# A seven-product feed-forward kernel: five couples of weight rows in each wide pair instead of four

## The reference

```python
f = jnp.square(jax.nn.relu(rms_norm(x, g_ffn_pre) @ w_up)) @ w_down
return x + rms_norm(f, g_ffn_post)
```

## Time and profile before

| | |
|---|---|
| median of 3 runs | 1889.78 us (1889.22 to 1890.29) |
| the profiled execution | 1889.38 us |
| its span | 1887.3 us |
| busy: PE, PE weight load, DVE, ACT | 99%, 89%, 79%, 59% |
| layer 0: feed-forward groups 0, 1, 2, 3 start their wide pairs at | 378.3, 539.8, 701.3, 863.2 us |

### The profile page before, as it was taken

One profiled execution on the slowest core, in us unless ns is written; L12 is line 12 of the kernel. 1 busy time (PEld: TensorE's weight loads), 2 busy tenths in 40 slices (PEclk: granted clock), 3 DMA queues, 4 the chain that ended last, 5 costly groups with the idle time before them and its releaser, 6 DMA issues.

```text
span 1887.3 us, 27369 instructions
## 1 busy us (share of the span) xinstructions
PE 1874.9 (99%) x9950; PEld 1672.1 (89%) x9950; DVE 1497.9 (79%) x1885; ACT 1111.4 (59%) x1485; POOL 118.5 (6%) x166
## 2 busy tenths in 40 slices
PE   9999999999999999999999999999999999999998
PEld 7988988988988998898888888889889889989987
DVE  6886657898699689788877757678977996897886
ACT  6455656855665565566554556568556655645662
POOL 3920010000000000000000000100000000000000
PEclk9999999999999999999999999999999999999999
DMA  8665366757566666767576554586676666567673
GB/s 290 201 221 181 112 201 226 236 182 255 189 198 216 214 198 195 236 202 241 210 234 225 187 168 134 170 275 194 197 236 207 195 212 221 183 207 235 221 257 124
DMA packets 170068, 390.92 MB, mean 207 GB/s; under 512 B 12161, under 2 KB 14321, under 8 KB 168433
## 3 DMA queue, kind: packets, MB, share of 16 engines
q1 hardware_dynamic: 167904, 377.58, 61.8%
q10 hardware_dynamic: 2064, 12.08, 1.7%
HBM read 382.53 MB, written 7.08 MB: 206 GB/s over the span
## 4 chain that ended last, share of the span: by engine, by line
PE 95%; DVE 3%; issue 1%; ACT 0%; DMA 0%; POOL 0%; DVEq 0%; POOLq 0%; ACTq 0%
PE acc_pair L573 25%; PE acc_pair L578 13%; PE acc_pair L539 8%; PE acc_pair L540 8%; PE acc_pair L541 8%; PE acc_pair L874 7%; PE acc_pair L873 7%; PE acc_pair L872 7%; DVE w_lo L1445 1%; PE t_bank L874 1%; PE t_bank L873 1%; PE t_bank L872 1%; PE o_bank L791 1%; DVE h_both L1501 1%; PE ssa_bank L872 1%
## 5 line engine op out<-in xcount | busy, mean ns | idle before, releaser
L995 ACT CAST w_hi<-raw 128x1024 fp32r<-128x1024 f32 x687 | 703.6, 1048 | 476.4 <-DVE raw L1998 190.7
L1445 DVE TENSOR_TENSOR w_lo<-raw,w_hi 128x1024 fp32r<-128x1024 f32 x687 | 827.4, 1232 | 169.0 <-ACT w_hi L995 161.8
L573 PE MATMUL acc_pair<-h_both,w_hi 128*128 128x512 f32 x2176 | 560.3, 380 | 0.2
L573 PEld LDWEIGHTS acc_pair<-h_both,w_hi 128*128 128x128 f32 x2176 | 371.4, 190 | 30.4 <-issue 0.5
L578 PEld LDWEIGHTS acc_pair<-h_both,w_lo 128*128 128x128 f32 x2176 | 327.4, 190 | 29.2
L578 PE MATMUL acc_pair<-h_both,w_lo 128*128 128x256 f32 x2176 | 330.5, 274 | 0.0
L872 PE MATMUL acc_pair<-w_hi,f_hi 128*128 128x512 f32 x504 | 191.0, 379 | 0.0
L873 PE MATMUL acc_pair<-w_lo,f_hi 128*128 128x512 f32 x504 | 191.0, 379 | 0.0
L874 PE MATMUL acc_pair<-w_hi,f_lo 128*128 128x512 f32 x504 | 191.0, 379 | 0.0
L539 PE MATMUL acc_pair<-w_hi,h_both 128*128 128x512 f32 x444 | 170.4, 384 | 1.8 <-DVE w_lo L1445 1.6
L540 PE MATMUL acc_pair<-w_lo,h_both 128*128 128x512 f32 x444 | 168.3, 379 | 0.0
(11 more groups left out here) (252 smaller groups left out, 2293.8 us busy)
## 6 DMA issues: line engine op xcount, KB each, us to landing
raw<-in_w_up SPq DMA_DIRECT2D x256, 512.0 KB, 4.4
raw<-in_w_down SPq DMA_DIRECT2D x240, 512.0 KB, 5.0
raw<-in_w_in SPq DMA_DIRECT2D x128, 512.0 KB, 4.7
raw<-in_w_out SPq DMA_DIRECT2D x64, 512.0 KB, 5.3
raw_side<-in_w_down SPq DMA_DIRECT2D x16, 512.0 KB, 7.0
x_kept<-x ACTq DMA_DIRECT2D x4, 1024.0 KB, 6.2
x<-x_kept ACTq DMA_DIRECT2D x4, 1024.0 KB, 6.1
x<-in_x SPq DMA_DIRECT2D x8, 256.0 KB, 7.5
```

The source lines that it names most:

```text
L573: pe.matmul(acc_pair[b][:, m, :], w_hi[:, slot, col:col + P], x_both.rearrange("p s (a n) -> p s n a", a=2), start=(slot, k) == (0, 0), st ...
L995: act.copy(w_hi[:, half * PAIRS + p, :], raw[:, p, :]).then_inc(hi_made, 1)
L1445: dve.tensor_tensor(w_lo[:, slot, :], src[:, p, :], w_hi[:, slot, :].bitcast(F32), ALU.subtract).then_inc(lo_made, 1)
```

## The change

Each wide pair has five couples of seven products and three plain ones. In the first pair of a group they are at slots 0, 4, 6, 10 and 12, in the second at 0, 4, 8, 12 and 14. Their activation rows come from up units 0 to 2, so there are no activation sums in the last unit, and one more set per group; in group 0 the sums of unit 0 are read from PSUM. The weight sums are formed by other formulas in another order: first the difference that goes back into `raw` (`weight_third`, now waiting for both loads), then one sum of 512 columns, then one subtraction 1024 wide. Where a couple follows a couple, `weight_third` of the next stands ahead of `t_lo`. The four shared banks are one tensor; in groups 0 and 1 ACT copies them out, in groups 2 and 3 DVE adds them in one instruction 2048 wide. In group 0 ACT also reads the banks of the first pair. In the last up unit DVE makes the second square, and prepares slots 0 to 5 instead of 0 to 7. At the end of a second pair the bank sums stand between low parts of the next unit.

```diff
-SEVEN_AT = (0, PAIRS, RING, RING + PAIRS)
-SEVEN_UNIT = ((1, 0), (1, 1), (2, 0), (2, 1))
-K_ORDER = (4, 5, 0, 1, 6, 7, 2, 3, 8, 9, 12, 13, 10, 11, 14, 15)
+SEVEN_AT = ((0, 4, 6, 10, 12), (0, 4, 8, 12, 14))
+COUPLES = tuple(len(at) for at in SEVEN_AT)
+LAYER_COUPLES = FF_GROUPS * COUPLES[0] + (FF_GROUPS - 1) * COUPLES[1]
+SEVEN_UNIT = ((0, 0), (0, 1), (1, 0), (1, 1), (2, 0))[:max(COUPLES)]
+PLAIN_LAST = tuple(SLOTS - 2 not in at for at in SEVEN_AT)
 SHARED = 4
+def k_order(q):
+    pairs = [4 * u + 2 * b for u, b in SEVEN_UNIT[:COUPLES[q]]]
+    plain, order = iter([k for k in range(0, KT, 2) if k not in pairs]), []
+    for i in range(0, SLOTS, 2):
+        k = pairs[SEVEN_AT[q].index(i)] if i in SEVEN_AT[q] else next(plain)
+        order += [k, k + 1]
+    return order
+K_ORDER = (k_order(0), k_order(1))
...
-    t_bank = [nc.alloc_psum_tensor(f"t_bank{n}", [P, CH], F32) for n in range(2)]
-    o_bank = nc.alloc_psum_tensor("o_bank", [P, CH], F32)
-    ssa_bank = nc.alloc_psum_tensor("ssa_bank", [P, CH], F32)
+    shared = nc.alloc_psum_tensor("shared", [P, SHARED, CH], F32)
+    ssa_bank, t_bank, o_bank = shared[:, 0, :], [shared[:, 1, :], shared[:, 2, :]], shared[:, 3, :]
...
-                    pe.wait_ge(lo_made, (hu + i // PAIRS) * PAIRS + 2 + RAW)
+                    pe.wait_ge(lo_made, (hu + i // PAIRS) * PAIRS + i % PAIRS + 2 + RAW)
...
-                        three(t_bank[1][:, :], sh[:, 0, :], sl[:, 0, :], th[:, 0, :], tl[:, 0, :],
+                        three(o_bank[:, :], sh[:, 1, :], sl[:, 1, :], th[:, 0, :], tl[:, 0, :],
                               begin, end).then_inc(t_used, 1)
-                        three(o_bank[:, :], sh[:, 1, :], sl[:, 1, :], th[:, 1, :], tl[:, 1, :],
+                        three(t_bank[1][:, :], sh[:, 0, :], sl[:, 0, :], th[:, 2, :], tl[:, 2, :],
                               begin, end).then_inc(t_used, 1)
                     if first:
...
-                          th[:, 2, :], tl[:, 2, :], first, False).then_inc(t_used, 1)
+                          th[:, 1, :], tl[:, 1, :], first, closing).then_inc(t_used, 1)
...
+                def two_hi(g, q, i):
+                    hu = hu0 + HU_F + g * HU_GROUP + 2 * CHUNKS + PAIR_HALVES * q + i // PAIRS
+                    if i in SEVEN_AT[q]:
+                        act.wait_ge(t_third, seven_no(l, g, q, SEVEN_AT[q].index(i)) + 1)
+                    split_hi(hu, i // PAIRS % 2, (i % PAIRS, i % PAIRS + 1))
+                def wide_hi(g, q, begin, end=SLOTS):
+                    for i in range(begin, end, 2):
+                        two_hi(g, q, i)
+                        if i in SEVEN_AT[q]:
+                            sums_hi(g, q, SEVEN_AT[q].index(i))
...
+                def first_shared(g):
+                    if g == 0:
+                        act.wait_ge(x_saved, 16 * T * (l + 1))
+                    act.wait_ge(t_used, 3 * seven_no(l, g, 0, COUPLES[0]) - 1)
+                    for k in range(SHARED):
+                        act.copy(kept_sums[:, 1 - pair_at(g, 0), k, :], shared[:, k, :]
+                                 ).then_inc(shared_free, 1)
...
+                def first_sums():
+                    act.wait_ge(rstd_ready, T + l * RS_LAYER + RS_X2 + T)
+                    for t in range(T):
+                        for c in range(2):
...
+                            dst = halves(acc[:, t, c_cols(2 * pair_at(0, 0) + c)])
+                            act.mul(dst, put_back(acc_pair[t][:, c, :]),
+                                    rstd[:, COL_X2 + t:COL_X2 + t + 1]).then_inc(acc_free[t], 1)
...
-                    seven_hi(g, 0, 2, hu + 10, 0)
-                    seven_hi(g, 0, 3, hu + 11, 1)
+                    last_unit(g)
+                    wide_hi(g, 0, 6)
                     if not last:
-                        for n in range(PAIR_HALVES):
-                            seven_hi(g, 1, n, hu + 12 + n, n % 2)
+                        wide_hi(g, 1, 0, 2)
+                        if g < T:
+                            first_shared(g)
+                        two_hi(g, 1, 2)
+                        if first:
+                            first_sums()
+                        wide_hi(g, 1, 4)
...
+                def last_square(g):
+                    z = act_f[:, 1, :]
+                    dve.wait_ge(acc_free[1], 1 + a0 + ACC_F + g * 8 + CHUNKS)
+                    dve.scalar_tensor_tensor(z, z, 0.0, z, ALU.max, ALU.mult
+                                             ).then_inc(f_ready, 1)
...
+                def weight_third(g, q, n):
+                    i = SEVEN_AT[q][n]
+                    hu = hu0 + HU_F + g * HU_GROUP + 2 * CHUNKS + PAIR_HALVES * q + i // PAIRS
+                    top_r, low_r = (raw[:, i % PAIRS + m, c_cols(1)] for m in range(2))
+                    for m in range(2):
+                        dve.wait_ge(raw_loaded[i % PAIRS + m], hu * 16 + 16)
+                    dve.tensor_tensor(top_r, low_r, top_r, ALU.subtract).then_inc(t_third, 1)
+                def weight_sums(g, q, n):
+                    no, i = seven_no(l, g, q, n), SEVEN_AT[q][n]
+                    top = raw[:, i % PAIRS, :]
+                    low = raw[:, i % PAIRS + 1, :].rearrange("p (c n) -> p c n", c=2)
+                    out = t_sum[t_buffer(q, n)]
+                    if q * COUPLES[0] + n > 1:
                         dve.wait_ge(t_used, 3 * no - 5)
+                    elif l + g > 0:
+                        dve.wait_ge(t_used, 3 * seven_no(l, g, 0, 0))
                     elif n == 1:
                         dve.wait_ge(tables_saved, 32)
-                    dve.wait_ge(raw_loaded[0], hu * 16 + 16)
-                    dve.tensor_tensor(out[:, 0, :], top_r, top_l, ALU.subtract
+                    dve.wait_ge(t_third, no + 1)
+                    dve.tensor_tensor(out[:, 0, :], top[:, c_cols(1)], top[:, c_cols(0)], ALU.add
                                       ).then_inc(t_step, 1)
-                    dve.wait_ge(raw_loaded[1], hu * 16 + 16)
-                    dve.tensor_tensor(top_r, low_r, top_r, ALU.subtract).then_inc(t_third, 1)
-                    dve.wait_ge(t_step, 3 * no + 1)
-                    if again:
-                        dve.wait_ge(t_used, 3 * no - 4)
-                    dve.tensor_tensor(out[:, 1, :], low_r, out[:, 0, :], ALU.subtract
-                                      ).then_inc(t_step, 1)
-                    dve.wait_ge(t_step, 3 * no + 2)
-                    if again:
+                    dve.wait_ge(t_step, 2 * no + 1)
+                    if q * COUPLES[0] + n > 1:
                         dve.wait_ge(t_used, 3 * no - 3)
-                    dve.tensor_tensor(out[:, 2, :], low_l, out[:, 1, :], ALU.subtract
-                                      ).then_inc(t_step, 1)
+                    dve.tensor_tensor(out[:, 1:3, :], low, out[:, 0:1, :].to_broadcast([P, 2, CH]),
+                                      ALU.subtract).then_inc(t_step, 1)
...
+                def couple_lo(g, q, i):
+                    n = SEVEN_AT[q].index(i)
+                    weight_sums(g, q, n)
+                    two_lo(g, q, i)
+                    if i + 2 in SEVEN_AT[q]:
+                        weight_third(g, q, n + 1)
                     sums_lo(g, q, n)
-                    split_lo(hu, half, (2, 3))
+                def wide_lo(g, q, begin):
+                    for i in range(begin, SLOTS, 2):
+                        if i not in SEVEN_AT[q]:
+                            two_lo(g, q, i)
+                            continue
+                        if i - 2 not in SEVEN_AT[q]:
+                            weight_third(g, q, SEVEN_AT[q].index(i))
+                        couple_lo(g, q, i)
...
-                    for k, bank in enumerate((ssa_bank, t_bank[0], t_bank[1], o_bank)):
-                        dst = kept_sums[:, 1 - j, k, :]
-                        if g < T:
-                            dve.tensor_copy(dst, bank[:, :]).then_inc(shared_free, 1)
-                        else:
-                            dve.tensor_tensor(dst, bank[:, :], dst, ALU.add
-                                              ).then_inc(shared_free, 1)
+                    dve.wait_ge(t_used, 3 * seven_no(l, g, 0, COUPLES[0]) - 1)
+                    dve.wait_ge(shared_free, shared_done(l, g - T))
+                    dst = kept_sums[:, 1 - pair_at(g, 0), :, :]
+                    dve.tensor_tensor(dst, shared[:, :, :], dst, ALU.add
+                                      ).then_inc(shared_free, SHARED)
...
-                    hu = hu0 + HU_F + g * HU_GROUP + 2 * CHUNKS + PAIR_HALVES * q
-                    seven_lo(g, q, 2, hu + 2, 0)
-                    seven_lo(g, q, 3, hu + 3, 1)
-                    nxt = hu + PAIR_HALVES
+                    nxt = hu0 + HU_F + g * HU_GROUP + 2 * CHUNKS + PAIR_HALVES * (q + 1)
+                    wide_lo(g, q, (6, 4)[q])
                     if q == 0 and not last:
-                        weight_sums(g, 1, 0, nxt)
```

(37 more changed lines are left out.)

209 lines of the change are left out of this document (115 added, 94 removed).

## The result

The changed kernel takes 1927.32 us (median of 4 runs, 1926.58 to 1931.76) against 1889.97 for the kernel before in the same session: a ratio of 1.0203, 95% interval 1.0185 to 1.0221. The sign was forecast, the size was not: +37 us where I had said +11, and outside my range. The profiled execution has a span of 1925.8 us, against 1887.3.

What follows compares the result with a forecast made beforehand. PE bounds the kernel (busy 99%), with DVE close behind. 9.1 us of matmuls go, DVE's lateness costs 10.2 us a layer, 20.4 in two: 1889.4 - 9.1 + 20.4 = 1900.7, about 1901; range 1881 to 1908.

Steps and rivals of the forecast that it cites:

- What goes: In 7 wide pairs of 2 layers, a fifth couple removes 42 matmuls of 0.2158 us: 9.1 us less on PE.
- What DVE gets: In wide pairs, each couple costs DVE 4.13 us; five with 16 low parts take 38.8 us against PE's 38.2.
- the sum: DVE's queue counted from PE's first matmul: group 1 ends at 75.4, 3.5 us late; overall 1889.4 - 9.1 + 20.4 = 1900.7.
- The waits for the landing: In two wide pairs, differences needing the second load wait 1.10 us at four places: 4.4 us.
- The first rival: Loads land within about 3.9 us of release, so the four waits vanish: 1882 us, chance 0.23.
- The rule in the Trainium skill: Load landing: about 2.0 us and bytes over 436e3, an estimated 3.2 us for 512 KB; the trace had 5.0.
- The lateness of PE by group: Feed-forward part: PE late by 0.9, 3.5, 5.0 and 0.4 us in groups 0 to 3; with starts, 10.2 a layer.
- Group 0: Two wide pairs without the bank sums: DVE done at 72.8, 0.9 us after PE wants it.
- Group 3: One wide pair: low parts, shared addition and two bank sums end at 38.6 against 38.2, 0.4 us late.
- The starts: At the next group's start, two bank sums stand ahead of the third low part: 0.4 us for a layer.
- The clock, assumed full: PE was at the full granted clock (2.4 GHz) in every slice; matmuls were priced at 0.2158 us throughout.
- The own range: 1892 to 1908: landing by 0.25 us each way moves 6 us, ACT's wait and the 1024-wide form 3 more.

Runs made afterwards that it cites:

- e11: The change with the old weight-sum order, s_hi behind ACT's DMA issues, four couples in first pairs and five in second ones: 1888.04 us.
- e4: The change with w_down loads in wide pairs bringing only the left half of each tile (256 KB), engine instructions unchanged: 1897.17 us.
- e13: The change with only the order and formulas of the weight sums put back to those of before: 1905.64 us.
- e8: The change with four couples in every wide pair and ACT's s_rest(0, 0) moved behind its four DMA issues: 1896.18 us.
- e12: The change, five couples in all pairs, with the old weight-sum order and ACT's s_hi behind its DMA issues: 1904.00 us.
- e15: Same as e12, but first pairs' couples at slots 0, 4, 6, 8, 12 (fourth couple moved earlier): 1923.91 us.
- e3: The change with four couples in first pairs (slots 0, 4, 8, 12) and five in second pairs: 1899.48 us.
- e7: The change with four couples in every wide pair and the second pair's bank sums behind all four low parts: 1906.47 us.
- e5: The change with the subtraction sums_lo (t_lo of the wide pairs' couples) made by POOL instead of DVE: 1990.86 us.

## Why the prediction was right in sign and wrong in size

**What goes.** Right: 42 matmuls of 0.2158 us. e11 keeps 18 of them, 3.9 us, and gains 2.2.

**What DVE gets.** Right within a tenth: the second couple's `t_lo` ended 7.7 us after PE's start (7.4 forecast), the 1024-wide subtraction is 1.14, the shared addition 2.2, the weight sums 2.66 against 2.46. The 0.2 is the difference standing directly ahead of the sum that reads it (579.15 - 578.36 = 0.79 and not 0.60). Five times in group 1's two pairs, that is 1.0 us: the last low part was done at 76.8 where the sum had 75.4.

**The waits for the landing.** Right in mechanism and price (0.84 to 1.14 against 1.10), shown by e4 and e13. The first rival, which hung on a landing of 3.9 us, fell: e4 reaches 3.0 only with half the bytes. The rule in the Trainium skill (DMA: Bandwidth & Descriptors, Anatomy of one DMA), by which I had an estimated 3.2 us for 512 KB, is fitted there to DMAs that GpSimd issues, which I had not said; SP issues the loads here. The trace shows a median of 4.8, and 3.0 for 256 KB. The measurement decides.

**The lateness of PE by group.** This is the step that failed. The sum had 10.2 us of it in a layer; the change shows 22.8 in layer 1 (the 18.3 above and the 4.5 of the saved matmuls). Four terms were wrong:

- *Group 0, 0.9 forecast.* PE waited 1.3 us at the start of the second pair for ACT's copies of the shared banks, and 1.4 for its last `w_lo`. I had priced the four copies (2.04 us in the trace) only as a delay of DVE's next low part, and not as what PE's `shared_free` waits for. Group 1 has the same wait with 0.9, and 1.1 more for the bank sums ahead of `acc_pair`, which I had named but not added.
- *Group 3, 0.4 forecast, 3.0 measured.* DVE stood for ACT's `w_hi` of the narrow part's slots, ahead of the shared addition and the banks:

```profile
912.00 1.23 DVE L1517 TENSOR_TENSOR w_lo<-raw,w_hi 128x1024 fp32r<-128x1024 f32 x1 [0.29 <-ACT w_hi L1028]
915.59 1.23 DVE L1517 TENSOR_TENSOR w_lo<-raw,w_hi 128x1024 fp32r<-128x1024 f32 x1 [2.36 <-ACT w_hi L1028]
916.73 2.28 DVE L2145 TENSOR_TENSOR kept_sums<-shared,kept_sums 128x2048 f32<-128x2048 f32 x1
```

  The sum had these low parts ready when DVE came. I counted DVE's own work and not the loads in front of it. The trace of before already had this wait, and there it cost nothing, because DVE was early enough to wait 1.41 us for PE behind it:

```profile
893.82 1.23 DVE L1445 TENSOR_TENSOR w_lo<-raw,w_hi 128x1024 fp32r<-128x1024 f32 x1 [2.50 <-ACT w_hi L995]
896.45 0.69 DVE L2035 TENSOR_TENSOR kept_sums<-ssa_bank,kept_sums 128x512 f32<-128x512 f32 x1 [1.41 <-PE o_bank L874]
```

  The loads of the narrow part land late: e4, which leaves them whole, has them apart from the wide pairs' with a median of 7.1 us, and PE still waits 2.18 and 1.96 us at this place there. From 912 to 918 us the change's DMA engines are busy all the time and move 396 GB/s.
- *The starts, 0.4 for a layer.* It is 0.55 for each of three groups. And the units of layer 0, costed at nothing, lost 1.7 to `s_hi` on ACT (e8; between e13 and e12 it is 1.6): a step on ACT that I never followed past DVE.
- *The clock, assumed full.* Behind the four longest waits it was not, and that is 6.7 us of the two layers. In group 2 of layer 1 it is nearly all that was missing: 5.5 + 1.3 = 6.8 us, of which the clock has 1.5, against 5.0 in the sum.

By the table these and the small ones are some 12 us a layer beyond the forecast, 24 in two, and with the 1.7 of layer 0 and the 1.2 that is the spread of executions the 27 us by which the profiled execution misses the sum.

**What is behind the first three** is that I took lateness at the end of a pair as the one quantity, and let each group's be the largest single deficit. But a late DVE is late for every reader in turn (shared banks, `acc_pair`, last couple, next unit), and PE's wait for one does not settle the next where DVE then waits for loads again.

**The own range**, 1892 to 1908, moved the known terms only. What was missing was not in any of its bounds, and the range that I gave, 1881 to 1908, has the same upper end.

**Left open:** why the waits are 1.0 in some places and 1.14 in others, and how the remaining 16 us of first pairs with five couples (e12 against e11) divide between the neighbouring couples, the bank work at their end and the clock; e15 tried one other placement, and it was worse for a reason of its own. What decides whether a wait is followed by the lower clock is open too.

## What to carry to other kernels

When two engines run neck and neck, the first instruction that reads a load decides how long that load is covered: an order of sums with fewer instructions but with both loads needed at once cost 21.7 us here, and nearly nothing (1.5) where the engine had room. Follow a late engine past its first late result, and list every reader that it serves, on every queue. A wait that costs nothing in the profile before may be one that only an early engine hides. And before moving work to a free engine, look whether it shares a port with the busy one.

## What the runs showed of the hardware

- Behind each of the change's four longest waits (2.99 to 3.97 us) PE's granted clock fell to its lower level for some 3.4 us (0.72 on average over the 6 us above), with matmuls 0.43 us apart. The longest wait so cost nearly half as much again as its own length (1.8 us on 3.97).
- The length of the wait alone does not decide it. In e12, at the same place of group 2, a wait of 2.64 us in layer 0 was followed by the full clock and one of 2.50 us in layer 1 by the lower one; in e3 one of 1.92 us (up to 781.53) was followed by the lower clock, and in e7 one of 3.48 us (up to 790.24) by the full one (e12's two windows, then e7's):

```profile
744.00:750.00 6.00, 4.94 (x22) 3.85 (x23) 6.00 (x8) 0.00 (x0) 0.00 (x0) 1.00 0.51 160
1684.00:1690.00 6.00, 3.50 (x10) 2.69 (x10) 6.00 (x6) 0.49 (x1) 0.00 (x0) 0.72 0.52 172
788.00:794.00 6.00, 3.76 (x22) 3.46 (x23) 6.00 (x8) 3.61 (x4) 0.00 (x0) 1.00 0.51 171
```

- A DVE subtraction of two SBUF inputs that starts during a POOL subtraction stands until POOL is done: 3.70 us for 0.69, 4.16 for 1.23, and so in all 70 cases of e5. Four DVE operations with one input in PSUM did not.
- A load of 512 KB landed after a median of 4.8 us and one of 256 KB after 3.0, in the same place of the program.
